# A two-block transformer kernel in split fp32: reordered steps on VectorE in both attentions, and squares added in pairs ahead of two norms

## What is computed

```python
# first block, one layer
h = rmsnorm(x, attn_norm_g)
fq, fk, fv, f_logit, sq, sk, sv = split(h @ w_in)      # 8 + 8 heads of 64
o = concat(rmsnorm(fox_attention(fq, fk, fv, log_sigmoid(f_logit + bias)), fox_out_g),
           rmsnorm(stick_breaking_attention(sq, sk, sv), sb_out_g))
x = x + o @ w_out
u = causal_dwconv(rmsnorm(x, ffn_norm_g) @ w_up)
x = rmsnorm(x + (silu(gate) * val) @ w_down, final_norm_g)
# second block, two layers; c is one vector
mod = silu(c) @ w_ada[i] + b_ada[i]                    # sh_m, sc_m, g_m, sh_f, sc_f, g_f
h = rms_norm(x, norm_mix[i]) * (1 + sc_m) + sh_m
y = moba_attention(h)  if i == 0 else  short_conv(h)   # 8 heads of 128, T = one block: causal softmax
x = x + g_m * y
h = rms_norm(x, norm_ffn[i]) * (1 + sc_f) + sh_f
x = x + g_f * (silu(h @ w_gate) * (h @ w_up)) @ w_down
```

## Time and profile before

| | |
|---|---|
| median of the runs shown | 910.61 us (909.53 to 910.64) |
| the profiled execution, its own time | 910.13 us |
| its span, first to last instruction | 908.5 us |
| mean granted TensorE clock | 0.999 of full speed |
| busy: TensorE / VectorE / ScalarE / POOL | 898.9 / 752.8 / 506.3 / 49.7 us |
| chain that ended last, by engine | PE 89%, DVE 7%, ACT 2% |
| splits on VectorE (L1038) | 292 of 1221 ns |
| splits on ScalarE (L598) | 291 of 1056 ns |
| accumulations (L1054) | 56, 114.2 us in all |
| matmuls L1731 (`act_hi`) | 1296 of 279 ns |
| read from memory | 205.75 MB, 228 GB/s over the span |

### The profile page before, as it was taken

The page is one execution under the profiler, slowest core; times in us unless marked ns, Lnnn a source line. Parts: engine busy times, 40 slices in busy tenths (PEclk is TensorE's granted clock), DMA queues, the critical chain, the costliest instruction groups (busy, mean ns, idle before and its releaser), DMA issues.

```text
span 908.5 us, 18262 instructions
## 1 busy us (share of the span) xinstructions
PE 898.9 (99%) x7351; PEld 874.6 (96%) x7351; DVE 752.8 (83%) x1043; ACT 506.3 (56%) x795; POOL 49.7 (5%) x87
## 2 busy tenths in 40 slices
PE   9999999999999999999999999999999999999998
PEld 8999999999999999899999999999999999999886
DVE  6999989999899799898987887987998887667544
ACT  6446757666665577664755445446545664544531
POOL 5100000000001000010000100100000000000000
PEclk9999999999999999999999999999999999999999
DMA  9887375676667948475469988984688477664541
GB/s 290 280 281 272 113 246 199 222 229 198 231 232 279 326 140 268 155 267 192 138 216 322 335 305 305 332 271 146 200 276 262 137 229 254 232 214 182 183 140 47
DMA packets 132129, 207.72 MB, mean 229 GB/s; under 512 B 4710, under 2 KB 109536, under 8 KB 126944
## 3 DMA queue, kind: packets, MB, share of 16 engines
q1 hardware_dynamic: 123968, 156.47, 51.0%
q0 software_dynamic: 8064, 50.34, 16.0%
q10 hardware_dynamic: 32, 0.01, 0.0%
HBM read 205.75 MB, written 1.05 MB: 228 GB/s over the span
## 4 chain that ended last, share of the span: by engine, by line
PE 89%; DVE 7%; ACT 2%; issue 1%; DMA 1%; SPq 0%; DVEq 0%; ACTq 0%
PE bank L1731 25%; PE bank L1733 25%; PE bank L1732 25%; PE bank L1888 2%; PE bank L1804 2%; PE bank L1802 2%; PE bank L1813 2%; DVE w_lo L1038 1%; PE bank L1776 1%; PE bank L1768 1%; PE bank L1770 1%; DVE ada_acc L1054 1%; ACT w_hi L598 1%; DMA x_in<-in_x 1%; PE bank L2209 0%
## 5 line engine op out<-in xcount | busy, mean ns | idle before, releaser
L1038 DVE TENSOR_TENSOR w_lo<-w_raw,w_hi 128x1024 fp32r<-128x1024 f32 x292 | 351.3, 1221 | 104.5 <-ACT w_hi L598 103.2
L598 ACT ACTIVATE w_hi<-w_raw 128x1024 fp32r<-128x1024 f32 x291 | 303.8, 1056 | 236.1 <-PE bank L1733 221.7
L1731 PE MATMUL bank<-act_hi,w_hi 128*128 128x256 f32 x1296 | 361.4, 279 | 0.1
L1732 PE MATMUL bank<-act_lo,w_hi 128*128 128x256 f32 x1296 | 358.3, 276 | 0.0
L1733 PE MATMUL bank<-act_hi,w_lo 128*128 128x256 f32 x1296 | 358.3, 276 | 0.0
L1731 PEld LDWEIGHTS bank<-act_hi,w_hi 128*128 128x128 f32 x1296 | 243.4, 188 | 0.7 <-issue 0.6
L1732 PEld LDWEIGHTS bank<-act_lo,w_hi 128*128 128x128 f32 x1296 | 243.5, 188 | 0.4 <-issue 0.2
L1733 PEld LDWEIGHTS bank<-act_hi,w_lo 128*128 128x128 f32 x1296 | 243.4, 188 | 0.0
L1054 DVE SCALAR_TENSOR_TENSOR ada_acc<-ada_raw,silu_c,ada_acc 128x2048 f32<-128x2048 f32 (+1 forms) x56 | 114.2, 2040 | 1.7 <-DMA ada_raw<-in_w_ada 1.4
L1731 PE MATMUL bank<-hid_hi,w_hi 128*128 128x256 f32 x352 | 98.2, 279 | 0.0
L1732 PE MATMUL bank<-hid_lo,w_hi 128*128 128x256 f32 x352 | 97.2, 276 | 0.0
(11 more groups left out here) (321 smaller groups left out, 1403.9 us busy)
## 6 DMA issues: line engine op xcount, KB each, us to landing
w_raw<-in_w_gate_up SPq DMA_DIRECT2D x44, 1024.0 KB, 5.1
ada_raw<-in_w_ada POOLq DMA_DIRECT2D x40, 1024.0 KB, 5.3
w_raw<-in_w_down SPq DMA_DIRECT2D x33, 1024.0 KB, 5.3
w_raw<-in_w_in SPq DMA_DIRECT2D x23, 1024.0 KB, 6.8
w_raw<-in_w_up SPq DMA_DIRECT2D x22, 1024.0 KB, 5.6
w_raw<-in_w_qkv SPq DMA_DIRECT2D x12, 1024.0 KB, 7.3
w_raw<-in_w_out SPq DMA_DIRECT2D x8, 1024.0 KB, 6.8
ada_raw<-in_w_ada POOLq DMA_DIRECT2D x16, 512.0 KB, 4.4
```

What stands on the lines that cost most here:

```text
L598: act.activation(unit(w_hi, u), raw_half(c, h), ACT.Copy).then_inc(hi_ready, 1)
L1038: dve.tensor_tensor(unit(w_lo, u), raw_half(c, h), unit(w_hi, u).bitcast(F32), ALU.subtract).then_inc(lo_ready, 1)
L1731: pe.matmul(dst, a_hi, b_hi, start=start, stop=False, skip_group_check=True)
L1732: pe.matmul(dst, a_hi, b_lo, start=False, stop=False, skip_group_check=True)
```

## The change

In the first attention the placing of chunk 1 moves from (1, 1) to (1, 0), and two accumulations from (11, 0) and (11, 1) to (11, 1) and (12, 0). In the second attention the accumulations get other slots, exponentials take the slots of the logits (two of them half a chunk earlier), the logits go ahead of the low part of an output, and the sum of piece 2 moves from behind the layer to (13, 1), ahead of the last head's low part. In norms 3 and 5 (`PAIRED`) VectorE adds the squares of tiles 2, 3 and then 4, 5 to those of tiles 0, 1 (`add_squares`), and TensorE sums two tiles in place of six there; ScalarE makes the mean and the square of 1/rms, VectorE the Newton step in two operations; both splits of the first normed chunk stand ahead of all low parts; and the splits around the updates stand elsewhere. In UP2 alone TensorE waits, ahead of the first normed chunk, for the completion of its own raw chunks. The diff, cut:

```diff
...
 SCORES2 = [(3, 0), (4, 0), (5, 0), (6, 0), (8, 0), (9, 0), (11, 0), (11, 1)]
 PROBS2 = [(4, 0), (5, 0), (6, 0), (7, 0), (9, 0), (10, 0), (12, 0), (12, 1)]
-EXPS2 = [(3, 1), (4, 0), (5, 0), (6, 1), (8, 0), (9, 0), (11, 0), (11, 1)]
 VALUES2 = [(5, 1), (6, 0), (8, 0), (8, 1), (11, 0), (11, 1), (12, 1), (13, 1)]
-ADA_AT1 = [(3, 0), (4, 0), (4, 1), (7, 0), (7, 1), (8, 0), (11, 0), (11, 1)]
+ADA_AT1 = [(3, 0), (4, 0), (4, 1), (7, 0), (7, 1), (8, 0), (11, 1), (12, 0)]
...
-ADA_AT2 = [(1, 0), (2, 0), (5, 0), (7, 0), (8, 0), (10, 0)]
+ADA_AT2 = [(3, 0), (5, 0), (6, 0), (8, 0), (9, 0), (10, 0)]
...
+PAIRED = (3, 5)
...
                     if raw:
-                        if j == 2 and n not in (2, 4):
+                        if j == 2 and n not in (2, 4) and n not in PAIRED:
                             split_unit(*late)
                         if j == 0 and n > 1:
                             act.activation(raw_hi[:, :, T:RAW_W], shifts(n), ACT.Copy)
-                        raw_upper(n, 2 * j)
-                        if (n, j) != (4, 2):
-                            raw_upper(n, 2 * j + 1)
+                        for k in ((), (0,), (1, 2, 3, 4, 5))[j] if n in PAIRED else (2 * j, 2 * j + 1):
+                            if (n, k) != (4, 5):
+                                raw_upper(n, k)
+                            if k == 3 and n in PAIRED:
+                                split_unit(*late)
...
+                if n in PAIRED:
+                    act.activation(n_a[:], bank[SUM_BANK[n]][:, 0:T], ACT.Identity, bias=eps[:], scale=1.0 / D
+                                   ).then_inc(y_mean, 1)
                 act.wait_ge(ln_ready, n)
                 act.activation(n_y[:], n_y[:], ACT.Exp, scale=-0.5).then_inc(y_ready, 1)
+                if n in PAIRED:
+                    act.wait_ge(y_ready, n)
+                    act.activation(n_t[:], n_y[:], ACT.Square).then_inc(y_sq, 1)
...
-                for h in heads_at(EXPS2, c, half):
+                for h in heads_at(SCORES2, c, half):
...
+            def root(n):
+                if n in PAIRED:
+                    dve.wait_ge(y_mean, PAIRED.index(n) + 1)
+                    dve.wait_ge(y_sq, PAIRED.index(n) + 1)
+                    link(dve.scalar_tensor_tensor(n_t[:], n_t[:], -0.5, n_a[:], ALU.mult, ALU.mult))
+                    link(dve.scalar_tensor_tensor(rstd[:], n_t[:], 1.5, n_y[:], ALU.add, ALU.mult))
+                    return
...
                 for k in range(KT):
                     part(k)
+                if n in PAIRED:
+                    split(c0 + 2)
                 for j in range(4):
-                    if c0 is not None and j % 2 == 0:
+                    if c0 is not None and n not in PAIRED and j % 2 == 0:
                         split_unit(c0 + 2, j // 2)
                     rest(j)
...
+                if n in PAIRED:
+                    add_up_paired(n, c0, gate, piece)
+                    return
...
+            def add_up_paired(n, c0, gate, piece):
+                def step(j):
+                    update(bank[OUT_BANKS[c0][j]], j, gate)
+                split_unit(c0 + 4, 0)
+                modulation(piece)
+                dve.wait_ge(unit_done, 2 * (c0 + 2) + 2)
+                step(0)
+                step(1)
+                dve.wait_ge(bank_done, BANKS_DONE[c0] + 1)
+                step(2)
+                add_squares(n, 0)
+                add_squares(n, 1)
+                split_unit(c0 + 4, 1)
+                dve.wait_ge(unit_done, 2 * (c0 + 3) + 2)
+                step(3)
+                raw_lower(n, range(KT))
+                split_unit(c0 + 5, 0)
+            def add_squares(n, later_pair):
+                dve.wait_ge(sq_ready, 5 * (n - 1) + 2 + later_pair)
+                if later_pair:
+                    dve.wait_ge(sq_added, 2 * PAIRED.index(n) + 1)
+                pair = slice(2 + 2 * later_pair, 4 + 2 * later_pair)
+                dve.tensor_tensor(scr[:, 0:2, :], scr[:, 0:2, :], scr[:, pair, :], ALU.add).then_inc(sq_added, 1)
...
-            EARLY = ((0, 1), (1, 1), (4, 1), (7, 1), (9, 1), (10, 1), (11, 1))
+            EARLY = ((0, 1), (1, 0), (4, 1), (7, 1), (9, 1), (10, 1), (11, 1))
...
-                    if h == 1 and c < 12 and (c, h) not in EARLY:
+                    if h == 1 and c < 12 and c != 1 and (c, h) not in EARLY:
...
             def attend2(c, half):
-                for h in heads_at(VALUES2, c, half):
-                    dve.wait_ge(o2_hi, h + 1)
-                    dve.tensor_tensor(ot_lo[:, h, :], bank[5 + h % 2][:, 0:T], ot_hi[:, h, :].bitcast(F32),
-                                      ALU.subtract).then_inc(o2_lo, 1)
                 for s in heads_at(SCORES2, c, half):
...
+                for h in heads_at(VALUES2, c, half):
+                    dve.wait_ge(o2_hi, h + 1)
+                    dve.tensor_tensor(ot_lo[:, h, :], bank[5 + h % 2][:, 0:T], ot_hi[:, h, :].bitcast(F32),
+                                      ALU.subtract).then_inc(o2_lo, 1)
...
+                    if (c, h) == (13, 1):
+                        fold_sum(2)
+                        attend2(c, h)
+                        split_unit(QKV + c + 2, h)
+                        continue
                     if (c, h) != (0, 0):
                         split_unit(QKV + c + 2, h)
...
-            fold_sum(2)
             add_up(OUT2, lambda k: mod[:, 0, G_M + k:G_M + k + 1], 2)
...
                             ins.then_inc(unit_done, 1)
-                        if n == 3 and outputs[0] == 2 and r < 1:
+                        if n == 3 and outputs[0] == 2 and r < 1 and NORM_AFTER[c0] not in PAIRED:
                             square_part(NORM_AFTER[c0], r + 2)
+                        if n == 3 and outputs[0] == 2 and r == 0 and NORM_AFTER[c0] in PAIRED:
+                            square_part(NORM_AFTER[c0], 0)
...
-                pe.wait_ge(sq_ready, 5 * (n - 1) + part + 1)
+                if part == 0 and n in PAIRED:
+                    pe.wait_ge(sq_added, 2 * PAIRED.index(n) + 2)
+                else:
+                    pe.wait_ge(sq_ready, 5 * (n - 1) + part + 1)
...
                     gate, val = pair_banks(p, i)
+                    if operand == 3:
+                        pe.wait_ge(unit_done, 2 * c)
                     chunk(c, gate, act_hi, act_lo, i, operand)
```

8 lines of the change are left out of this document (5 added, 3 removed).

## The result

| | before | with the change |
|---|---|---|
| median of 20 runs | 910.37 us | 917.91 us |
| lowest to highest | 909.53 to 913.67 | 905.51 to 919.07 |
| profiled execution, its own time | 910.13 us | 918.83 us |
| its span, granted clock | 908.5 us, 0.999 | 917.1 us, 1.00 |

The ratio of the change to the kernel before is 1.0046 (95% interval 1.0028 to 1.0063): slower by 0.5%, where a median of 906.4 us, within 904.6 to 908.6, was forecast. The ratio is smaller than that of the medians because the 20 times do not lie in one place. They fall in three heaps (groups of times with nothing between them): 4 at 905.5 to 906.2, 4 at 911.4 to 912.0, and 12 at 917.6 to 919.1. The 20 runs of the kernel before are one heap with one run at 913.67.

A forecast was written before the change was run, and what follows sets the result against it. TensorE bounds the kernel: matmuls fill 898.9 of 908.5 us. Terms -0.66 + 0.72 - 2.28 - 1.17 - 1.17 + 0.30 = -4.26 us take the profiled 910.13 to 905.9; plus 0.48, median 906.4, range 904.6 to 908.6.

The forecast's parts named there:

- so I charge nothing for the clock: End of the sum: clock row nine tenths or more in every slice, mean 0.999 of 2.4 GHz, so no time added.
- First scores: Chunk 1, first layer: keys placed ahead of one split, so TensorE starts scores earlier; gain 0.66 us, allowed 0.4 to 0.7.
- First attention: Its end: 0.41 us gained at the first output chunk, new wait of about 1.1 us at the transposes; loss 0.72 us.
- The rival without the new wait: First attention: VectorE reaches the token normalization in time, 0.72 loss becomes 0.41 gain, median 905.3 us; chance 0.15.
- Second attention: Moved accumulations and earlier exponentials remove waits of TensorE; gain 2.28 us, bounds 1.0 to 2.5.
- The three places forecast: Second attention: waits shortened or removed for probabilities at 364.31, before 380.73, and for the value copy at 387.73 us.
- The wait near 371: Second attention: the wait before 371.36 us (0.37 idle) was to stay and move along.
- Norms: Paired norms 3 and 5: 1.72 us of matmuls saved, less 0.55 for a wait and restart; gain 1.17 us each.
- The stop in UP2: TensorE's wait for its own raw chunks ahead of the first normed chunk; cost 0.30 us, between 0 and 0.65.
- Rival, VectorE as bound of the normed chunks: Slack of 0.35 us at the fourth chunk vanishes, most of both norms' 2.3 us given back, 908.3 us; chance 0.25.
- Rival, the early exponentials: Second attention: they hold ScalarE ahead of the squares; the place costs 2.2 us, median 910.9 us; chance 0.05.
- The sign of being wrong: Matmul count falls by 8 (16 passes) and time by less than 2 us, or the transposes start without a wait.

The follow-up runs named there:

- e3_attn: The edits in both attentions alone, norms as before, no stop in UP2, against the kernel before: median 910.0 us, ratio 0.9992.
- e1_again: The same program as the change, run once more for a second profile and more times: median 912.6 us, ratio 1.0041 to the kernel before.

## Why the prediction was wrong

- **What bounds the kernel.** Right that only TensorE counts, and wrong in "only two things can shorten this kernel: fewer matmuls, or shorter waits". Time per matmul is a third, and it moved by 12.8 us where those two moved by 4.3.
- **The step that failed** is in the sum: "so I charge nothing for the clock". The clock was rightly left out, since it is 1.00 in every window at either pace, but with it I took for granted that the matmuls behind each edit follow one another every 0.1133 us as before. The sum put this term at nothing without a reason, and it measured 12.8 us. No rival had the matmuls themselves slower. The kernel before shows the slow pace in short stretches of its attentions (five of 42 to 44 matmuls between 342 and 409 us, two more near 10 and 121 us), and I had read matmul rows only where TensorE waited.
- **First scores:** mis-sized. I had written that the DMA's two rows "are not seen landing" and yet set the lower bound at 0.4. It measured 0.21; the wait's releaser is that DMA.
- **First attention:** right in mechanism: 0.64 us were gained from the first scores to the first output chunk (0.41 forecast), and 1.08 lost at the transposes (1.13 forecast). That the whole, 0.78, comes so near to 0.72 is luck, since 0.33 of it is slow pace in OUT1. The rival without the new wait falls.
- **Second attention:** 2.61 against 2.28 (e3_attn). The three places forecast gave 0.89, 0.32 and 1.14 (0.90, 0.23 and 1.15 forecast); the rest lies near 341 us (0.10) and near 392 us (0.17), where I forecast nothing. The wait near 371 stayed (0.65 between starts, as before).
- **Norms:** 1.20 and 1.21 against 1.17; the wait for the added squares opened 0.60 us between starts in both. The stop in UP2 cost 0.32 against 0.30.
- **Rival, VectorE as bound of the normed chunks:** its slack was overrated for norm 5: 0.35 was forecast, 0.3 is found in UP2 of e1_again and 0 in its UP3. Its price was of another kind than I said: 9 ns of lateness, and 4.1 us of slow pace behind it.
- **Rival, the early exponentials:** fell; no wait near 355 to 390 but the one at 371.
- **The range:** its lower end, 904.6, is not "all bounds on the good side". These add up to -0.7 - 0.41 - 2.5 - 1.72 - 1.72 + 0 = -7.05, which gives 903.6.
- **The sign of being wrong** that was named came true: 16 passes less, and the time not 2 us lower but 7.5 higher. It points at the sum as a whole and not at the pace.
- The times that belong to the sum (905.5 to 906.2) are 4 of 20 runs, and the median is 12 us above.
